# Expert feed-forward of a two-layer trunk: gate and up panels in pairs with 512-column matmuls, activations transposed on VectorE, down panels in 8 KB rows, a hinted back edge for TensorE's loop

## What is computed

```python
def swiglu(h, w_gate, w_up, w_down):
    return (jax.nn.silu(h @ w_gate) * (h @ w_up)) @ w_down

def moe_swiglu(h, w_router, w_gate, w_up, w_down):
    ...
    logits = (t @ w_router).astype(jnp.float32)
    top_v, top_i = lax.top_k(logits, TOP_K)
    gates = jax.nn.softmax(top_v, axis=-1)
    comb = jnp.sum(jax.nn.one_hot(top_i, N_EXPERTS, dtype=jnp.float32) * gates[..., None], axis=1)
    ...
    for e in range(N_EXPERTS):
        out = out + comb[:, e:e + 1] * swiglu(t, w_gate[e], w_up[e], w_down[e])
```

## Time and profile before

| | us |
|---|---|
| median of 3 runs | 1739.5 (1734.86 to 1746.77) |
| the profiled execution, whole | 1740.47 |
| its span | 1738.5 |
| before the first expert matmul (layer 0, delta rule, routing) | about 722 |
| head and seven iterations of the loop | 722 to 1629 |
| last expert, combination, final norm | 1629 to 1738.5 |

### The profile page before, as it was taken

How to read it: one execution, slowest core, us unless ns; L and a number is a source line. 1 busy time by engine, 2 the same in 40 slices (tenths; PEclk the granted TensorE clock), 3 DMA queues, 4 the chain that set the end, 5 groups by cost and what they waited for, 6 DMA issues and landing times.

```text
span 1738.5 us, 49245 instructions
## 1 busy us (share of the span) xinstructions
PE 1617.2 (93%) x22767; PEld 1212.5 (70%) x22767; DVE 464.7 (27%) x767; ACT 394.9 (23%) x699; POOL 171.7 (10%) x168
## 2 busy tenths in 40 slices
PE   8899999989999988999999899899899899899997
PEld 7789998877878767766566576576576566566665
DVE  5654544483849473400000000000000000000003
ACT  5444343554545353100000000000000000000000
POOL 0100000142525232000000000000000000000000
PEclk9799999999999999999999999999999999999999
DMA  9146555443222001999989999999899898899990
GB/s 348 52 155 207 176 183 181 146 146 98 73 99 73 25 1 49 412 391 387 357 330 373 358 350 352 340 358 363 329 380 366 330 391 340 322 390 358 387 402 31
DMA packets 159273, 452.33 MB, mean 260 GB/s; under 512 B 9920, under 2 KB 41184, under 8 KB 159072
## 3 DMA queue, kind: packets, MB, share of 16 engines
q1 hardware_dynamic: 155536, 437.10, 67.6%
q0 software_dynamic: 3536, 12.06, 1.8%
HBM read 441.79 MB, written 7.34 MB: 258 GB/s over the span
## 4 chain that ended last, share of the span: by engine, by line
PE 85%; DVE 5%; issue 4%; ACT 3%; POOL 1%; SPq 1%; DMA 1%; DVEq 0%; POOLq 0%; ACTq 0%
PE bank L1890 30%; PE bank L1920 17%; PE bank L1418 8%; PE bank L1419 7%; PE bank L1420 7%; PE bank L1905 5%; PE bank L1935 2%; PE bank L1809 1%; PE bank L1819 1%; POOL qdec L529 1%; DMA par<-in_attn_sinks_dram 1%; ACT whi L615 1%; DVE TT L1205 1%; DVE cvall L1114 1%; PE bank L1801 0%
## 5 line engine op out<-in xcount | busy, mean ns | idle before, releaser
L1890 PE MATMUL bank<-ring,xg 128*32 128x256 f32 x9216 | 518.2, 384 | 1.1
L1890 PEld LDWEIGHTS bank<-ring,xg 128*32 128x32 f32 x9216 | 322.8, 111 | 189.4 <-issue 22.5
L1920 PE MATMUL bank<-ring,ehT 128*32 128x256 f32 x5376 | 298.8, 379 | 0.6 <-ACT ehT L858 0.6
L1920 PEld LDWEIGHTS bank<-ring,ehT 128*32 128x32 f32 x5376 | 188.6, 110 | 100.8 <-issue 1.3
L1418 PE MATMUL bank<-whi,xhi 128*128 128x256 f32 (+1 forms) x688 | 223.9, 325 | 7.5 <-DVE oall L1092 2.1
L1419 PE MATMUL bank<-wlo,xhi 128*128 128x256 f32 (+1 forms) x688 | 218.2, 317 | 0.0
L1420 PE MATMUL bank<-whi,xlo 128*128 128x256 f32 (+1 forms) x688 | 218.1, 317 | 0.0
L1249 DVE TENSOR_TENSOR ehid<-bank,esil 128x512 f32<-128x512 f32 x24 | 16.6, 691 | 733.7 <-PE bank L1890 733.7
L934 DVE TENSOR_TENSOR wlo<-raw,whi 128x2048 fp32r<-128x2048 f32 x74 | 177.7, 2403 | 79.4 <-ACT whi L615 79.0
L615 ACT CAST whi<-raw 128x2048 fp32r<-128x2048 f32 x74 | 141.0, 1906 | 51.2 <-PE bank L1420 46.4
L1418 PEld LDWEIGHTS bank<-whi,xhi 128*128 128x128 f32 x688 | 131.9, 192 | 20.5 <-issue 4.2
(11 more groups left out here) (317 smaller groups left out, 1497.2 us busy)
## 6 DMA issues: line engine op xcount, KB each, us to landing
ring<-in_moe_w_gate_dram SPq DMA_DIRECT2D x112, 1024.0 KB, 7.4
ring<-in_moe_w_up_dram SPq DMA_DIRECT2D x112, 1024.0 KB, 7.2
ring<-in_moe_w_down_dram SPq DMA_DIRECT2D x112, 1024.0 KB, 7.6
raw<-in_dn_w_in_dram SPq DMA_DIRECT2D x24, 1024.0 KB, 5.3
raw<-in_ffn_w_gate_dram SPq DMA_DIRECT2D x11, 1024.0 KB, 5.4
raw<-in_ffn_w_up_dram SPq DMA_DIRECT2D x11, 1024.0 KB, 5.5
raw<-in_ffn_w_down_dram SPq DMA_DIRECT2D x11, 1024.0 KB, 4.9
raw<-in_dn_w_o_dram SPq DMA_DIRECT2D x8, 1024.0 KB, 5.0
```

Of the source, the lines that this page charges most:

```text
L1890: last = pe.matmul(token_tile(2 * m, t, q, 256), xg[:, kt, TILE * t:TILE * (t + 1)], w[:, at_:at_ + 256], start=kt == 0 and t % 2 == 0, st ...
L1920: i = pe.matmul(token_tile(4, t, q, 256), ehT[:, h_:h_ + TILE], w[:, at_:at_ + 256], start=first and m == 0 and k == 0 and t % 2 == 0, sto ...
```

## The change

Gate and up panels are now loaded and used alternately, in pairs. `gate_up` waits for both panels of a pair and gives strips 0 and 1 of the array to the gate panel, strips 2 and 3 to the up panel, with 512 moving columns a matmul (two runs of 256) into one whole bank for each token tile (banks 0 to 2). So gate results stand in partitions 0 to 63 and up results in 64 to 127. For the half chunk the same function runs with 256 columns. A pair of wide panels is 24 matmuls (48 pairs of instructions), where two panels were 48 (96).

ACT's Silu waits for the whole chunk, reads partitions 0 to 63 of three banks in one instruction (3 x 512 elements a partition) and writes `esil` on partitions 64 to 127. DVE multiplies on those 64 lanes in two instructions of 768 elements, each reading its operands with a step of 8 elements (4 in the half chunk), and then transposes `ehid` in 32x32 blocks into one of two `ehT` buffers. PE's transposes and ACT's copies of them are gone; at their place PE only waits for `ehid`. The unit order that the block transposes give is met by loading the down panels with the row split (p k): a partition's two rows of a panel lie side by side, one piece of 8 KB, at a step of 32 KB between partitions in the wide chunks (16 KB in the half one). PE's loop carries a prefetch hint for its back edge. Some small buffers move.

```diff
-    psum = [nc.alloc_psum_tensor(f"bank{n}", [P, 512], F32) for n in range(8)]
-    bank = [b[:, :] for b in psum]
+    psum = nc.alloc_psum_tensor("banks", [P, 8 * 512], F32)
+    bank = [psum[:, n * 512:(n + 1) * 512] for n in range(8)]
+    products = psum[:, 0:TILES * 512].rearrange("p (t c) -> p t c", t=TILES)
...
-    esil = at("esil", TILES * 256, W0 + 54)
+    esil = at("esil", TILES * 512, W0 + 36)[:, :].rearrange("p (t c) -> p t c", t=TILES)
     ehid = at("ehid", TILES * 256, W0 + 57)
-    ehT = at("ehT", 2 * TILES * P, W0 + 60)
+    ehT = [at(f"ehT{n}", TILES * 256, W0 + 60 + 3 * n) for n in range(2)]
...
-                sp.dma_start(expert_slot(n)[:, :].rearrange("p (k n) -> p k n", k=src.shape[1] // P),
-                             src.rearrange("a (k p) n -> p (a k) n", p=P)).then_inc(landed[(n - P_MOE) % RING], 16)
+                sp.dma_start(expert_slot(n)[:, :].rearrange("p (k n) -> p k n", k=src.shape[1]), src)\
+                    .then_inc(landed[(n - P_MOE) % RING], 16)
...
-                    w = (e_gate, e_up)[i % 8 // 4]
-                    expert_panel(P_MOE + i, in_rows(w, 0, i // 8, i % 4))
+                    expert_panel(P_MOE + i, in_rows((e_gate, e_up)[i % 2], 0, i // 8, i % 8 // 2))
...
-                    for i in range(2 if c == ECH - 1 else 4):
-                        r = c * 1024 + i * 256
-                        panel_of(at_ + i, down_rows[bass.ds(e * FFE + r, 256), :].unsqueeze(0))
+                    n = 4 if c == ECH - 1 else 8
+                    s_ = down_rows[bass.ds(e * FFE + c * 1024, n * P), :].rearrange("(p k) n -> p k n", k=n)
+                    for i in range(n // 2):
+                        panel_of(at_ + i, s_[:, 2 * i:2 * i + 2, :])
...
             def silu(used, wide_):
+                n_ = 512 if wide_ else 256
                 act.wait_ge(panel_used, used)
-                if wide_:
-                    act.activation(esil[:, 0:512], bank[0], ACT.Silu)
-                    i = act.activation(esil[:, 512:768], bank[1][:, 0:256], ACT.Silu)
-                else:
-                    i = act.activation(esil[:, 0:384], bank[0][:, 0:384], ACT.Silu)
-                i.then_inc(sem("esil_ready"), 1)
-
-            def hidden_sb(u, wide_):
-                act.wait_ge(sem("ehT_psum"), u + 1)
-                if wide_:
-                    act.copy(ehT[:, 0:512], bank[6])
-                    i = act.copy(ehT[:, 512:768], bank[7][:, 0:256])
-                else:
-                    i = act.copy(ehT[:, 0:384], bank[6][:, 0:384])
-                i.then_inc(sem("ehT_ready"), 1)
...
+            def hidden(u, even, wide_, earlier_=True):
+                k_, n_ = (8, 512) if wide_ else (4, 256)
+                by_row = lambda t, s: t[64:P, :, s * n_ // 2:(s + 1) * n_ // 2].rearrange("p t (j k) -> p t k j", k=k_)
+                eT = ehT[0 if even else 1]
                 dve.wait_ge(sem("esil_ready"), u + 1)
-                dve.wait_ge(panel_used, used)
-                if wide_:
-                    dve.tensor_tensor(ehid[:, 0:512], bank[2], esil[:, 0:512], ALU.mult)
-                    i = dve.tensor_tensor(ehid[:, 512:768], bank[3][:, 0:256], esil[:, 512:768], ALU.mult)
-                else:
-                    i = dve.tensor_tensor(ehid[:, 0:384], bank[2][:, 0:384], esil[:, 0:384], ALU.mult)
+                if earlier_:
+                    dve.wait_ge(sem("ehT_ready"), u)
+                for s in range(2):
+                    i = dve.tensor_tensor(ehid[64 * s:64 * s + 64, 0:TILES * n_ // 2].rearrange("p (t k j) -> p t k j", t=TILES, k=k_),
+                                          by_row(products, s), by_row(esil, s), ALU.mult)
                 i.then_inc(sem("ehid_ready"), 1)
+                dve.wait_ge(sem("ehid_ready"), u + 1)
+                dve.transpose(eT[:, 0:TILES * n_ // 2], ehid[:, 0:TILES * n_ // 2]).then_inc(sem("ehT_ready"), 1)
...
+            def gate_up(n0, done, first, end, wide_=True):
+                k_, n_ = (2, 512) if wide_ else (4, 256)
+                for i in range(first // 2, end // 2):
+                    w = []
+                    for n in (n0 + 2 * i, n0 + 2 * i + 1):
+                        pe.wait_ge(*expert_landed(n, done))
+                        w.append(expert_slot(n)[:, :].rearrange("p (k s h c) -> p k s h c", k=k_, s=2, h=2))
+                    for k in range(k_):
+                        kt = k_ * i + k
                         for t in range(TILES):
                             for q in range(4):
-                                at_ = k * 1024 + q * 256
-                                last = pe.matmul(token_tile(2 * m, t, q, 256), xg[:, kt, TILE * t:TILE * (t + 1)], w[:, at_:at_ + 256],
-                                                 start=kt == 0 and t % 2 == 0, stop=kt == KT - 1, skip_group_check=t % 2 == 1)
-                    last.then_inc(panel_used, 1)
-
-            def gate_up_half(n0, done, first, end):
-                for j in range(first, end):
-                    m, i = divmod(j, 2)
-                    n = n0 + j
-                    pe.wait_ge(*expert_landed(n, done))
-                    w = expert_slot(n)
-                    for k in range(4):
-                        kt = 4 * i + k
-                        for t in range(TILES):
-                            for q in range(4):
-                                at_ = k * 512 + q * P
-                                last = pe.matmul(token_tile(2 * m, t, q, P), xg[:, kt, TILE * t:TILE * (t + 1)], w[:, at_:at_ + P],
-                                                 start=kt == 0 and t == 0, stop=kt == KT - 1, skip_group_check=t > 0)
-                    last.then_inc(panel_used, 1)
-
-            def down(n0, done, u, m0, m1, wide_, first, last):
+                                last = pe.matmul(bank[t][TILE * q:TILE * (q + 1), 0:n_].rearrange("p (s c) -> p s c", s=2),
+                                                 xg[:, kt, TILE * t:TILE * (t + 1)], w[q // 2][:, k, :, q % 2, :],
+                                                 start=kt == 0, stop=kt == KT - 1)
+                    last.then_inc(panel_used, 2)
...
-                            h_ = (2 * t + k) * P + TILE * m if wide_ else t * P + TILE * (2 * m + k)
+                            h_ = (t * (8 if wide_ else 4) + 2 * m + k) * TILE
...
+            def hidden_done(u):
+                pe.wait_ge(sem("ehid_ready"), u + 1)
...
-            def hidden_T(u, wide_):
-                pe.wait_ge(sem("ehid_ready"), u + 1)
-                for k in range(2 * TILES if wide_ else TILES):
-                    i = pe.transpose(bank[6 + k // 4][:, k % 4 * P:(k % 4 + 1) * P], ehid[:, k * P:(k + 1) * P], ident)
-                i.then_inc(sem("ehT_psum"), 1)
...
             def body(it, last):
-                hidden_T(it * ECH, True)
+                hidden_done(it * ECH)
                 gate_up(B_MOE + G1, it, 0, 8)
                 pe.wait_ge(sem("yrow_ready"), it + 1)
-                down(B_MOE + D0, it, it * ECH, 0, 3, True, True, False)
+                down(B_MOE + D0, it, it * ECH, True, 0, 3, True, True, False)
...
-            with pe.Fori(0, final) as it:
+            with nc.Fori(0, final, engines=[pe.engine], hint_back_edge=True) as it:
```

More of the change, by code:

```diff
@@ L902, in _ @@
             gathered_sb(0)
-            silu(P_MOE + 4, True)
+            silu(P_MOE + 8, True)
             act.wait_ge(sem("npass_ready"), 1)
@@ L1877, in token_tile @@
                 return bank[first + at_ // 512][TILE * q:TILE * (q + 1), at_ % 512:at_ % 512 + width]
-            def gate_up(n0, done, first, end):
-                for j in range(first, end):
-                    m, i = divmod(j, 4)
-                    n = n0 + j
-                    pe.wait_ge(*expert_landed(n, done))
-                    w = expert_slot(n)
-                    for k in range(2):
-                        kt = 2 * i + k
+            def gate_up(n0, done, first, end, wide_=True):
[7 more added lines that the diff above has]
+                        kt = k_ * i + k
@@ L1909, in down @@
-            def down(n0, done, u, m0, m1, wide_, first, last):
+                                last = pe.matmul(bank[t][TILE * q:TILE * (q + 1), 0:n_].rearrange("p (s c) -> p s c", s=2),
+                                                 xg[:, kt, TILE * t:TILE * (t + 1)], w[q // 2][:, k, :, q % 2, :],
+                                                 start=kt == 0, stop=kt == KT - 1)
+                    last.then_inc(panel_used, 2)
+            def down(n0, done, u, even, m0, m1, wide_, first, last):
@@ L1982, in body @@
                     row_numbers()
-                down(B_MOE + D1, it, it * ECH + 1, 0, 4, True, False, False)
+                down(B_MOE + D1, it, it * ECH + 1, False, 0, 4, True, False, False)
                 if not last:
                     pe.wait_ge(sem("numbers_read"), it + 2)
-                hidden_T(it * ECH + 2, True)
-                gate_up_half(B_MOE + G3, it, 0, 4)
+                hidden_done(it * ECH + 2)
```

(7 more changed lines are left out.)

54 lines of the change are left out of this document (22 added, 32 removed).

## The result

The changed kernel takes 1667.0 us in the median of four runs (1665.8 to 1670.0), before 1740.7 in four: ratio 0.958, interval 0.954 to 0.962. The forecast was 1642 with a range of 1630 to 1682. So direction and range held, and the likeliest case (1630 to 1655) did not: 74 us were gained of the 97.5 forecast, so a quarter is missing. The profiled execution has a span of 1666.2 us.

What follows compares the result with a forecast made beforehand. PE was taken as the bound, with DMAs held back by it. Span 1738.5 - 96 (seven iterations) - 4 (last expert) + 2.5 (ahead of the loop) = 1640.5, giving a median of 1642 us, range 1630 to 1682.

Steps and rivals of the forecast that it cites:

- the likeliest case: Whole kernel: PE stays the bound near 112.5 us an iteration, 1630 to 1655 us, chance 0.70.
- Transposes: PE's activation transposes in each loop iteration go entirely, saving 2.9 us.
- Half chunk: Gate and up of the half chunk takes 10.5 us for 14.4, as fewer instructions are asked for.
- 512 columns: Wide gate and up matmuls: width itself gains nothing; 192 pairs take 20.6 to 20.74 us.
- Back edge: PE's jump to the loop's start: the hint cuts the 5.20 us hole to 0.4 and removes the half clock behind.
- G1: First gate and up stage of an iteration, right behind the back edge; taken as 21.2 us.
- a hint that hides only part: Rival at the loop's back edge: 1655 to 1665 us; hint wholly or partly useless has chance 0.12.
- Sum of an iteration: All PE stages of one loop iteration plus the edge: 112.5 us against 126.2.
- The wait ahead of the loop: PE waits 3.7 us instead of 1.21 for the uncovered activation chain; plus 2.5 us with clock loss.
- Cover of D3: An iteration's last down stage, 5.3 us, hides the 3.7 us activation chain; rival that it fails: 1655 to 1669, 0.06.
- DMAs: Expert loop: floor 111.8 us an iteration, PE barely stays the bound; rival of a 375 GB/s limit: 1684, 0.06.
- the slow rival: Wide down panels: 8 KB pieces at a 32 KB step fall on few memory channels; about 1880 us, chance 0.03.

Runs made afterwards that it cites:

- experiment 10: Changed kernel with every gate and up matmul issued as two of half the columns, same panels; no kernel time given, half chunk 16.0 us.
- experiment 2: Changed kernel with the hint and the loop's first instruction on slot 0 of a fetch block; 1633.9 us, ratio 0.945 to the kernel before.
- experiment 6: Changed kernel with the hint and the loop head on slot 72 of its fetch block; 1630.0 us, ratio 0.938 to the kernel before.
- experiment 7: Changed kernel with the hint and the loop head on slot 128 of its fetch block; 1673.8 us in one run.
- experiment 8: Changed kernel with the hint and the loop head on slot 108 of its fetch block; 1636.9 us in one run.
- experiment 3: Changed kernel with the hint marked just ahead of the iteration's last down stage instead of at the body's top; 1667.7 us, ratio 0.963.
- experiment 9: Kernel before with only the hint added on PE's loop; 1698.3 us, ratio 0.977.
- experiment 11: Changed kernel with hint and slot 72, down panels in 4 KB pieces and VectorE multiplying without the step, output not the reference's; 1630.0 us, ratio 0.936.
- the unrolled kernel: Changed kernel with PE's seven iterations written out one after the other, so no back edge; 1627.8 us, ratio 0.942 to the kernel before.
- experiment 12: Changed kernel with hint and slot 72, plus matmuls on idle banks in two waits of PE; 1631.8 us, ratio 0.936.

## Why the prediction was right, and where it was not

**Transposes** (minus 2.9 us an iteration): right, none is left and nothing took their place. **Half chunk** (10.5 for 14.4): right, 10.48; experiment 10 shows that the cause is the number of instructions. The 14.4 was the shortest of the seven before, whose mean is 14.9 us, so the change gained more here than was said; the sum started from the mean iteration and is not touched by it. **512 columns** (nothing by themselves): right, 20.60 for 20.74.

**Back edge** (0.4 us, with G1 at 21.2): this step failed. Measured are 8.8 to 11.0 us from D3 to G1 at six edges, where D3 alone is 5.18, and G1 at 22.2 to 22.8. The stages D3 at the edges sum to 56.2 us, 25.1 over six times 5.18, where the forecast had 2.4. G1 at the edges is 7 us over the 21.2 that were taken. The reason given ("the hint is there for exactly this fetch") took an instruction's purpose for its effect. The bounds, 0 and 5.2 us, held for the mean hole (4.0 us; the longest was 5.7), and the choice at the low one was made with no row. What the runs showed in its place: the hinted fetch comes no earlier than a packet that goes with the entry into the branch's own block, so a hinted edge costs what is left of about 6 us at the branch, 4.6 us here and 0.4 only when the branch stands late in its block (experiments 2, 6, 7 and 8). The rival of a hint that hides only part, 1655 to 1665, is in essence what happened (1667, 2 us above its band), and the median lies in the forecast range because that range had been left wide enough to take this rival in. Its mechanism was not the one that the prediction named (later blocks replacing what was fetched); experiment 3 speaks against it. The Trainium skill ("Runtime: NRT & Kernel Launch", Instruction fetch mechanics) states that prefetch is purely sequential. These traces do not agree: by that rule a hint could do nothing, and experiments 6 and 9 bring the taken branch to 0.36 us.

**Sum of an iteration** (112.5): 110.8 without the edge (experiment 6), so the other stages were 1.3 us too dear, mostly G1 (20.6 for 21.2) and the down stages (10.38 for 10.5). **Over the span:** the forecast span was 1640.5, measured 1666.2. The seven iterations took 813.7 us (745.60 to 1559.29) instead of 787.5: plus 22.7 of holes, plus 8.9 in G1 with its half clock (the first one, at 23.1 us, included), minus 5.4 in the other stages. Beside that stand plus 1.1 in the wait ahead of the loop, minus 1.6 in the last expert (89.9 us), plus 2.9 in the end, most of it a combination at half clock, and minus 3.3 ahead of the experts, which is no effect of the change.

**The wait ahead of the loop** (plus 2.5 us): too low. From the first row_numbers to the loop's first matmul it is 16.4 us instead of 12.8, plus 3.6; PE's wait there went from 1.21 to 4.85 us. The chain took 4.9 us, not 3.7: the Silu 1.44 us as forecast, but each multiplication 1.57 instead of 0.97.

**Cover of D3:** it held, with less to spare than thought. At the first back edge, DVE had multiplied by 858.57 (timeline of DVE: 855.40 plus 3.17), D3 ended near 859.0 and G1 began at 862.88. So DVE was not what PE waited for, and at slot 72, where nothing else delays G1, PE waited for DVE nowhere in the loop. The step of 32 bytes did cost: 1.6 times an element's time, where the rival needed more than twice to open a hole.

```profile
855.40 3.17 DVE L1237 TENSOR_TENSOR ehid<-banks,esil 64x768 f32<-64x768 f32 x2 [30.34 <-ACT esil L848]
858.60 0.98 DVE L1241 STREAM_TRANSPOSE ehT<-ehid 128x768 f32<-128x768 f32 x1
```

**DMAs** (PE stays the bound, barely): right. The floor put at 111.8 us an iteration was too high: at slot 72 an iteration ran in 110.8 with no landing waited for, 407 GB/s. So the 375 GB/s at a share of 1.00 in the earlier trace rows was no limit, as argued. In the profile after, the down panels landed 8.6 us after their issue, gate and up panels after 9.0 and 9.6, so the 32 KB step singled nothing out; and it cost nothing that reached the time (experiment 11), so the slow rival falls too.

## What to carry to other kernels

Price a prefetch hint by where the branch stands in its fetch block, not by its presence: read the duration of the closing branch in the trace, and try the loop's head at another slot. Here one line separates 1667 from 1630 us, ratios 0.958 and 0.938 to the kernel before. Any edit that changes the number of instructions moves the branch, so parts of a change are not additive at a back edge. And a stall named issue in a stage of short matmuls can be cured by fewer, wider instructions, even if a column costs the same, as the half chunk was.

## What the runs showed of the hardware that was not expected

A hinted branch is cheap only late in its block. With the head on slots 0, 72, 108 and 128 the six taken back edges take 1.5, 0.37, 0.37 and 5.9 us in the median; without the hint 6.2 to 6.9. That the fetch is triggered when the branch's own block is entered explains their order, the jump and the packets' starts; the entry into a block itself is not recorded, and at slot 0 the rule with 5.8 us and 128 to 147 slots would leave 1.8 to 2.3 us, a little more than measured.

Leaving a hinted loop has a price if the branch stands late in its block. At slot 72 the last expert shows a hole that the unrolled kernel does not have:

```profile
1524.10 17.80 PE L1875 MATMUL banks<-ring,xg 128*32 128x512 f32 x164 [2.42 <-issue]
```

At slot 108 the hole at the same place is 4.84 us, and on the kernel before the hint alone brings one of 3.26 us where there was none. In the six profiles with such a hole a packet of the instruction queue starts 3.9 to 5.0 us after the branch that is not taken, and PE goes on 2.3 to 2.6 us after that packet's start. That fits a fetch of the loop's head in place of the code that follows the loop. Between three kernels with the head on slot 72 the hole varied from 1.9 to 3.3 us (experiments 6, 11 and 12), so differences of their expert stages under 2 us say little.

A DVE multiplication of one PSUM and one SBUF operand takes 0.96 us for 64x768 elements read in order and 1.57 us read with a step of 8. The Trainium skill ("SBUF — State Buffer", Door 1: The DMA port swizzle) states a penalty for crossing its 16-byte lines; the sign agrees, and the size here is a factor of 1.6. Both operands, in PSUM and in SBUF, were read with the step, so which of them pays is not shown. A DVE transpose of 128x768 floats in 32x32 blocks takes 0.98 us. Whether the half clock follows a short hole varied between executions: behind the same 1.0 us of waiting the combination took 7.8 to 8.2 us in three profiles (after and experiments 3 and 7) and 5.35 in ten others.
